# Three taps of a long convolution move behind the first units of the next product, and a wait ahead of nine transposes moves behind the seventh

## The reference, cut to what matters

```
u = x @ w_in                                   # [256, 20480]; columns: GLU | q | k | v | cb, cc, ch | gates
a = a_val * sigmoid(a_gate)
a = causal_depthwise_conv(a, conv_a_w) + conv_a_b      # 31 taps, 1024 channels
a = silu(layer_norm(a))
att = dilated window attention, 3 groups x 8 heads, merged by softmax weights
c = cb * causal_depthwise_conv(cc * ch, conv_c_w)      # 3 taps
proj = [a, att, c] @ w_branch;  merged = sum(sigmoid(g) * proj);  x1 = LN(alpha * x + merged @ w_out)
```

## Time and profile before

| | us |
|---|---|
| three runs | 2228.35, 2230.35, 2240.71 |
| their median | 2230.35 |
| the profiled execution, its own time | 2228.8 |
| its span, first to last instruction | 2227.0 |
| PE busy in it | 2195.0 (99%) |
| DVE busy | 1043.6 (47%) |
| ACT busy | 706.5 (32%) |
| POOL busy | 50.3 (2%) |
| read from memory | 640 MB, at 418 GB/s from 1260 to 2200 us |

### The profile page before, as it was taken

One profiled execution on the slowest core, in us unless ns is written; L12 is line 12 of the kernel. 1 busy time (PEld: TensorE's weight loads), 2 busy tenths in 40 slices (PEclk: granted clock), 3 DMA queues, 4 the chain that ended last, 5 costly groups with the idle time before them and its releaser, 6 DMA issues.

```text
span 2227.0 us, 34444 instructions
## 1 busy us (share of the span) xinstructions
PE 2195.0 (99%) x14150; PEld 1696.2 (76%) x14150; DVE 1043.6 (47%) x1331; ACT 706.5 (32%) x785; POOL 50.3 (2%) x56
## 2 busy tenths in 40 slices
PE   8999999999999999999999999999999999999997
PEld 7888888888888888888889666665666666666663
DVE  5444559996585666666665322222221112221224
ACT  4333543434444444444433211111111111111112
POOL 0000000000000000000100000000000000000000
PEclk9999999999999999999999999999999999999999
DMA  8555445556345655555677799999999999999996
GB/s 267 188 189 189 143 161 188 188 181 197 114 157 187 203 191 190 187 185 181 222 270 291 309 421 422 422 422 395 420 422 423 422 422 422 422 422 422 422 421 259
DMA packets 250670, 643.42 MB, mean 289 GB/s; under 512 B 5173, under 2 KB 185397, under 8 KB 198378
## 3 DMA queue, kind: packets, MB, share of 16 engines
q1 hardware_dynamic: 249578, 635.61, 75.0%
q0 software_dynamic: 880, 6.32, 0.8%
q10 hardware_dynamic: 144, 0.52, 0.1%
HBM read 640.34 MB, written 2.10 MB: 288 GB/s over the span
## 4 chain that ended last, share of the span: by engine, by line
PE 91%; DMA 6%; DVE 1%; issue 0%; ACT 0%; DVEq 0%; SPq 0%; ACTq 0%
PE ps_proj L1545 22%; PE ps_proj L1765 18%; PE ps_proj L1546 11%; PE ps_s L1804 9%; DMA ring<-in_w_up_dram 6%; PE ps_s L1536 4%; PE ps_t L1712 3%; PE ps_t L1820 3%; PE ps_proj L1820 2%; PE ps_proj L1712 2%; PE ps_s L1538 2%; PE ps_s L1519 2%; PE ps_t L1519 2%; PE ps_proj L1674 1%; PE ps_t L1520 1%; PE ps_s L1520 1%
## 5 line engine op out<-in xcount | busy, mean ns | idle before, releaser
L1545 PE MATMUL ps_proj<-x_both,w_both 128*128 128x512 f32 x2144 | 746.8, 393 | 0.0
L1546 PE MATMUL ps_proj<-x_both,w_both 128*128 128x256 f32 x2144 | 599.3, 280 | 0.0
L962 DVE TENSOR_TENSOR w_both<-raw,w_both 128x2048 fp32r<-128x2048 f32 x196 | 472.0, 2408 | 206.5 <-ACT w_both L673 206.0
L1545 PEld LDWEIGHTS ps_proj<-x_both,w_both 128*128 128x128 f32 x2144 | 402.0, 187 | 89.5
L1765 PE MATMUL ps_proj<-ring,xt 128*64 128x256 f32 x4160 | 456.0, 379 | 2.7 <-DMA ring<-in_w_up_dram 1.6
L1765 PEld LDWEIGHTS ps_proj<-ring,xt 128*64 128x64 f32 x4160 | 300.7, 137 | 166.0 <-issue 19.5
L1546 PEld LDWEIGHTS ps_proj<-x_both,w_both 128*128 128x128 f32 x2144 | 405.2, 189 | 0.1
L673 ACT ACTIVATE w_both<-raw 128x2048 fp32r<-128x2048 f32 x196 | 373.4, 1908 | 88.6 <-PE ps_proj L1546 41.7
L1804 PE MATMUL ps_s<-ring,ht 128*64 128x512 f32 x1056 | 233.9, 596 | 0.6 <-ACT ht L840 0.6
L1315 DVE SCALAR_TENSOR_TENSOR hidden<-ps_proj,slot_w,gate_sig 128x256 f32<-128x256 f32 x33 | 16.0, 484 | 363.7 <-ACT gate_sig L835 352.2
L1323 DVE TENSOR_TENSOR y_lo<-ps_s,y_hi 128x1024 fp32r<-128x1024 f32 x64 | 75.4, 1219 | 219.7 <-ACT y_hi L853 219.7
(11 more groups left out here) (294 smaller groups left out, 2304.4 us busy)
## 6 DMA issues: line engine op xcount, KB each, us to landing
raw<-in_w_in_dram SPq DMA_DIRECT2D x79, 2048.0 KB, 8.7
ring<-in_w_up_dram SPq DMA_DIRECT2D x64, 2048.0 KB, 19.9
ring<-in_w_down_dram SPq DMA_DIRECT2D x64, 2048.0 KB, 14.6
ring<-in_w_gate_dram SPq DMA_DIRECT2D x62, 2048.0 KB, 17.1
raw<-in_w_branch_dram SPq DMA_DIRECT2D x12, 2048.0 KB, 8.0
raw<-in_w_out_dram SPq DMA_DIRECT2D x8, 2048.0 KB, 9.3
first_gate<-in_w_gate_dram SPq DMA_DIRECT2D x2, 2048.0 KB, 14.9
ring<-in_w_gate_dram SPq DMA_DIRECT2D x4, 1024.0 KB, 20.6
```

The source lines that it names most:

```text
L962: nc.vector.tensor_tensor(split_lo(u, w), raw_half(u, w), split_hi(u, w).bitcast(F32), ALU.subtract).then_inc(s_lo, 1)
L1545: pe.matmul(sums[:, :], hi[:, t, :], x_both[:, :, t, :], start=(t == 0), stop=False)
L1546: ins = pe.matmul(sums[:, 0:TOK], lo[:, t, :], x_hi[:, t, :], start=False, stop=(t == KT - 1))
```

## The change

Taps 21 to 30 are spread otherwise. Before, the four units of the first group of `v1` carried taps 21 to 24, and the first three units of the two other groups 25 to 27 and 28 to 30. After, the first three units of the first group carry 21 to 23, the first two units of the others 24, 25 and 26, 27, and the first three units of `cc` carry 28, 29 and 30.

In `turn_probs` the wait for `s_att` is taken from ahead of the first transpose of each of the two sets and put ahead of the fifth of the second set (m == 4), the first that writes the bank of the result. It is left out for the very first head.

```
                 if name == "qk1" and (j == 3 or not first):

                     conv_tap(4 * i + j - 3, first)
-                if name == "v1" and first:
+                if name == "v1" and first and j < 3:
                     conv_tap(21 + j, False)
-                if name == "v1" and not first and j < 3:
-                    conv_tap(25 + 3 * (i - 1) + j, False)
+                if name == "v1" and not first and j < 2:
+                    conv_tap(24 + 2 * (i - 1) + j, False)
+                if name == "cc" and first and j < 3:
+                    conv_tap(28 + j, False)
...
                     if n >= 2:

                         pe.wait_ge(s_pt, n - 1)
-                        pe.wait_ge(s_att, 2 * (HALF * half + head))
                     for m in range(3 * kt):
+                        if kt == 2 and m == 4 and HALF * half + head:
+
+                            pe.wait_ge(s_att, 2 * (HALF * half + head))
                         ins = pe.transpose(turned_p[kt - 1][:, m * P:(m + 1) * P], att_p[kt - 1][:, m * P:(m + 1) * P],
                                            ident[:, :])
```

## The result

| | before | after |
|---|---|---|
| five runs each, us | 2228.2, 2228.35, 2228.48, 2230.35, 2240.71 | 2239.73, 2239.85, 2239.95, 2243.97, 2244.27 |
| median | 2228.48 | 2239.95 |
| profiled execution | 2228.8 | 2244.27 |
| PE busy | 2195.0 | 2213.2 |

The ratio is 1.0048, with a 95% interval of 1.0034 to 1.0062. The forecast was 2226.7 us, with a range of 2222.5 to 2233. The changed kernel lost some 11 us where 3.6 were to be won.

The account below looks back on a forecast made before the run. PE, busy 99%, was taken to bound the kernel, with DVE the bound of the v1 stretch. Taps 2.05 us plus the turn_probs wait 1.56 us gave 3.61 us, from 2230.35 to 2226.7 us; range 2222.5 to 2233 us.

Parts of the forecast that it names:

- The waits of the taps: PE's two waits in the v1 pairs for DVE's weight split, 2.5 us in all, would go.
- the 0.2 us to spare: Where a v1 group begins, DVE's path takes 10.85 us against a PE pair of 11.09, so no wait.
- The term was sized at 2.05: Moving taps from v1 to cc: 3.50 us lead won, 1.45 given back at c2, the third cc unit.
- the bound of 1.35: Gain in us from moving the taps if a slow pace stays in the v1 pairs, taking 0.7 us.
- The wait in turn_probs: Last head's transposes start 0.78 us earlier, in aval and in cc: 1.56 us won, moved wait costing nothing.
- without the wait there is no slow pair: The 2% slower v1 pairs behind the two waits vanish with them; if not, 0.7 us is lost.
- (a): The wait only moves: c2 starts at 14.8 us instead of 12.75, moving taps wins nothing, 2228.8 us; 12%.
- (b): Both gains whole, as c2 doesn't wait: 5.1 us won, 2225.3 us; 8%.
- (d): Slower: ACT's eviction of c0, held behind POOL's clearing, becomes the bound; 2232 us at 6 to 7 us hand-over; 3%.
- ACT's hold: ACT's eviction of c0 waits for POOL's c_pad clearing, done at about 10.7 us, hidden ahead of DVE's 12.08.
- (c): The clock falls to half rate behind the new wait at c2: only 1.9 us won, 2228.4 us; 7%.

Follow-up runs that it names:

- e2: Kernel before with only the wait in turn_probs moved, old taps kept: median 2240.25 us, ratio 1.0027.
- e6: Kernel before with only the wait in turn_probs moved, run again on another chip: median 2243.04 us, ratio 1.0056.
- e17: Kernel before with mixer matmuls ordered two of 512 columns, then two of 256: median 2231.39 us, ratio 1.0003 to the kernel before.
- e18: Changed kernel with mixer matmuls ordered two of 512 columns, then two of 256: median 2229.09 us, ratio 0.9990 to the kernel before.
- e5: Changed kernel, unaltered, run again on another chip: median 2242.12 us, ratio 1.0056 to the kernel before.
- e16: Changed kernel with one more, already satisfied wait on PE ahead of its first transpose: median 2240.86 us, ratio 1.0021 to the kernel before.

## Why the prediction was wrong

**The waits of the taps: right.** Both are gone, with the 0.2 us to spare. c2 came 12.67 us after c0 (12.75), and the idle time there was 1.19 us. Its worth was 86.99 - 86.24 = 0.75 us between the two traces, the one in mixed steps and the other in the slow one. Against e2 and e6, which have the old taps in nearly the same steps (87.4 and 87.2 us), it is 1.0 to 1.2 us, and 1.5 us in the order of two and two. The term was sized at 2.05. In the slow step it lies nearer the bound of 1.35 that I had worked out for a slow pace that stays.

**The wait in turn_probs: right, for itself.** 0.74 us in `aval` and 0.82 to 0.90 in `cc`, 1.56 us foretold. The transposes started 2.00 us after `values`, and the moved wait cost nothing where it stands.

**The failed step: "I take it that without the wait there is no slow pair".** I had seen the slow step, 11.41 and 11.39 us against 11.09, measured it at 2%, admitted that I didn't know its cause, and then priced it at 0.7 us, as a thing that hangs on a wait and ends with the pair. The runs showed in its place a state in which the mixer's products can run for hundreds of microseconds, with no wait near: the four stretches that turned slow fill 910 us of the kernel before, so the same 2% is 8.7 us in one of them and 17.4 us in all. With one step for all (e17 and e18), the two parts won 3.2 of the 3.6 us of the sum. A question left open at 2% of a pair had to be asked of the whole kernel, and no rival of mine did so. All of them, and the range, held PE's pace outside the touched places fixed.

**The rivals.** (a), (b) and (d) didn't happen: c2 came 12.67 us after c0 where 12.75 was foretold (14.8 in (a)), it did wait, and ACT's hold stayed hidden. ACT's eviction of c0 ended 10.58 us after c0 began (10.7 foretold), ahead of DVE's at 12.10:

```profile
546.07 0.39 ACT L702 ACTIVATE c_pad<-ps_proj 128x256 f32<-128x256 f32 x1 [5.73 <-POOL c_pad L606]
```

(c) was the nearest in kind, PE at another speed behind a disturbance, but by another mechanism. The granted clock was 1.00 in every window above where the slow step ran, and from 547 to 560 us of the changed kernel, behind c2's wait. On that point the Trainium skill, "TensorE: Matmul & The Clock Gate", Part 1, is neither borne out nor contradicted: the wait of 1.19 us at c2 brought no half rate.

**The range** took three runs on one chip for the spread of the kernel, and ended at 2233 us although one of the three had taken 2240.71. On the five chips of the experiments its runs lie between 2226.3 and 2246.0 us; its traces, of 2228.80 and 2237.39 us, differ in which stretches are slow. So the loss isn't a constant either: against a kernel before that drew mostly the fast long stretch it was measured as 0.5% (1.0048, and 1.0056 for e5), against one that drew both as 0.2 to 0.3% (e2, the wait alone, 1.0027; e16, the change with one more wait, 1.0021).

**What stays open.** Shown is that the step has two values, that a push of 0.2 us at the break ahead of the long stretch changes its value, and that with the wait moved in `cc` and nothing put at `cb` it was the slow one in all six traces and, by the times, in all 43 runs. How it does so is not. Some 53 us of other work lie between the attention of `cc` and `cb`. That `ch` ran there in one of two patterns, and that the pattern goes with the step behind it in all 16 traces, says that what carries over is PE's timing, to some nanoseconds. Whether that is its phase against the other engines or against its own weight loads I can only argue, and why the moved wait always ends in the second pattern is open. Why the first stretch, which nothing of the change precedes, was slow in most traces with a slow long stretch is open too, and so is why chips differ in how often the kernel before draws which. Not tried were longer pauses at the breaks and a break in every unit.

## What to carry to other kernels

Before pricing a wait of a microsecond in a kernel that is PE-bound for a millisecond, compare PE's pace: count the matmuls in equal windows, or take the distance between the starts of the same matmul in two traces. Busy time, the list of waits and the granted clock all miss a 2% slower step, and a wait moved behind seven transposes can bring it. And before a gain of 0.2% is believed, run the kernel before often enough, on more than one chip, to see how many levels it has.

## What the hardware showed that was not expected

- A steady stream of a 512 and a 256 column fp32 matmul, each with its own 128-column weight load, runs in a step of either 0.347 us or 0.353 us, at a granted clock of 1.00; the same stretch took 454.60 or 463.33 us in each of the 16 traces of that order, within a hundredth. The slow one repeats every three steps.
- Once entered, the slow step held for up to 540 us on end (463.33 + 78.79 after). A step put off by 0.1 us was enough for a change: from fast to slow at 1102 us in five traces, from slow to fast at 495 us in the kernel before. In e6 it changed with no such sign.
- The fast step has two patterns of the same mean (512-column matmuls of 394 or 391 ns in `ch`). Which of them ran there went with the step of the stretch behind the next break in all 16 traces, and one unread transpose at that break turned it round.
- The order 512, 512, 256, 256 has a single step of 0.348 us, 0.5% over the fast and 1.4% under the slow one.
- One unread 128-column transpose at a break, which put the next matmul off by 0.2 us (3.48 us behind the start of the channel sum instead of 3.26), took some 9 us off the median of a kernel, and in another kernel two such moved most runs the other way.
